# Sums of squares and the spreading of norms placed on column and row tiles of 32

## The chip, the cores and the metric

The kernel runs on one core of one Trainium2 chip, whose engines are TensorE (PE; its weight loads are shown as PEld), VectorE (DVE), ScalarE (ACT), GpSimd (POOL) and SyncE (SP, which issues the large transfers). The metric is device time in microseconds, from the launch to the end of the program. A profiled execution also has a span, from its first to its last instruction.

## The reference, cut to what matters

Three layers follow one another on 256 tokens of width 2048, in fp32. Each is a projection into a wide matrix, a mixer, and a projection back. The first layer's mixer is half sparse attention and half an RWKV recurrence of 16 heads of 64. The second is differential attention with 16 heads, each with two pairs of queries and keys of 64. Three places compute a norm over 64 neighbouring channels, and these are the ones that the change touches:

```python
# layer 1, RWKV: length of the keys, once for each head
kk = (k * k_k.astype(f32)).reshape(B, S, H, N)
kk = kk / jnp.maximum(jnp.sqrt(jnp.sum(kk * kk, axis=-1, keepdims=True)), 1e-12)
...
# layer 1, RWKV: group norm of the output, once for each head
mean = jnp.mean(y, axis=-1, keepdims=True)
var = jnp.mean(jnp.square(y - mean), axis=-1, keepdims=True)
y = ((y - mean) * lax.rsqrt(var + RWKV_GN_EPS)).reshape(B, S, W) * ln_w + ln_b
...
# layer 2: norm of 32 query vectors and 32 key vectors of 64 for each token
q = _rmsnorm(q.reshape(B, S, H, 2, d), qk_g[0]) * (d ** -0.5)
k = _rmsnorm(k.reshape(B, S, H, 2, d), qk_g[1])
```

## The kernel before

Activations lie with channels on partitions and tokens along the free dimension, so a tile is 128 channels by 256 tokens and holds two heads of 64. A norm over 64 channels is therefore a sum over half the partitions, and TensorE makes it. Each of the three norms goes the same way:

1. ACT squares the tiles.
2. **The sums** (`half_sums`, line 98). One matmul for each tile takes a 128-row window of a constant as its stationary operand (all ones in one column for partitions 0 to 63 and in the next column for 64 to 127, zeros elsewhere) and the squares as its moving operand. Shifting the window by two columns puts the sums of tile n in output rows 2n and 2n + 1. The matmuls of one norm accumulate in the same rows of one PSUM bank: 8 rows for the four tiles of RWKV, 32 rows for the 16 tiles of layer 2.
3. DVE and ACT turn these few rows into reciprocal roots: 8 or 32 partitions by 256 elements.
4. **The spread** (lines 970, 1109 and 1670). One matmul for each tile takes a selector (`chosen`, 0 or 1) as its stationary operand, 8 or 32 rows by 128 columns, and the reciprocals as its moving operand. It copies the two rows of that tile to the 128 partitions of its channels.
5. DVE multiplies the tiles by what lies in PSUM (lines 1295, 1395 and 1813).

The selectors are made at run time: POOL copies parts of the identity, each column repeated 64 times, into `chosen` (lines 1460 and 1472 in RWKV, 1917 in layer 2).

Each fp32 matmul appears in the trace as two LDWEIGHTS and two MATMUL instructions, so four such matmuls are a group of x8.

Around this runs the projection (class `Gemm`), which is most of TensorE's work. Weights come by transfers of 512 KB into `w_raw` (issued by SP, line 199, each when DVE has freed a buffer). ACT rounds them to `w_hi` (line 208), DVE makes the rest `w_lo` (line 213), and TensorE multiplies in three steps (lines 241 to 243, or 250 to 252 for the other layout), 256 columns each. TensorE's order is written out by hand: `merged` and `woven` insert the stages of the mixer between slots of the projection, where a slot is three of its matmuls and the lists `stage_slots` and `second_slots` say after which slot a stage comes. ACT and DVE have the same lists. Every engine works through its own order and waits on semaphores.

In RWKV the work comes in two halves (`hh` 0 and 1) of four tiles. `pe_prepare` has the sums of the keys' squares (line 964), the spread (970), the product for the bonus (976) and transposes (987). `pe_finish` has the means (1097), the sums (1102) and the spread (1109). After the second half's last step POOL sets `half_done`, for which SP waits before it loads the weights of the sparse half (line 407).

In layer 2 the function `sums` is called once for each of 16 pairs of tiles, `spread` likewise. Calls 0 to 7 are the queries, 8 to 15 the keys. `roots` on DVE makes the reciprocals of each half. Spreads 8 to 15 follow one another with three slots between them, in `ps` banks 2 and 3 by turns.

Other lines that the text names work on parts of the array already. Lines 1701 and 1702 are the scores of layer 2 with a contraction of 64: the matmuls for one head's t = 0 read partitions 0 to 63 and write bank 0, those for t = 1 read partitions 64 to 127 and write bank 1. Line 2168, in layer 3, has 64 output rows: its blocks b = 0 and 2 (256 and 128 columns) write partitions 0 to 63, b = 1 and 3 (192 and 64 columns) write 64 to 127, with two matmuls for each block. Lines 931 and 932 are two single matmuls, 33 rows by 8 columns into partitions 32 to 39 and 32 rows by 16 columns into partitions 0 to 15.

Of the kernel before, what the change touches and what calls it, by code (L numbers as in the profile page):

```python
# [21 lines left out]
P = 128  # L22
# [34 lines left out]
K_WIN1 = K_WIN2 + 126  # L57
K_END = K_WIN1 + 31

# [7 lines left out]
def constants():  # L67
# [14 lines left out]
    cols.append(np.broadcast_to(np.arange(31) == 15, (P, 31)))  # L82
# [696 lines left out]
def first_layer(k, a, g, xt, following):  # L779
# [14 lines left out]
    small, chosen = ar[0:8, 4096:4352], ar[0:8, 4352:4864]  # L794
    eight = view(con[0:8, K_ID:K_ID + 1], [[1, 8], [0, 64]])
# [13 lines left out]
    def bonus(hh):  # L809
        return k.proj[:, T_ZA:T_ZA + 4, :] if hh == 0 else raw(1, 0)  # L810
# [64 lines left out]
    with ExitStack() as ctx:  # L875
# [13 lines left out]
        f1, f2, th, ug, sg, sc_, md, ce, exd, e1, kr, s2, ss, nr, rn, nb, sl, kn, ka, bo, bp, bn, x1, tq, ev = semaphores(  # L889
            nc, ctx, "rwp", "f1 f2 th ug sg sc md ce ex e1 kr s2 ss nr rn nb sl kn ka bo bp bn x1 tq ev")  # L890
# [16 lines left out]
        def spread(u):  # L907
            return chosen[:, u * P:(u + 1) * P]
# [34 lines left out]
        def pe_prepare(pe, hh):  # L943
# [31 lines left out]
            for q in range(2):  # L975
                mm = pe.matmul(k.ps[:, 2 + q, :], blk, weighted[:, 2 * q:2 * q + 2, :], start=True, stop=True)
# [116 lines left out]
        def pe_finish(pe, hh):  # L1093
# [7 lines left out]
            for u in range(4):  # L1101
                mm = half_sums(k, pe, u, 8, k.ps[0:8, 2, 0:S], ep(hh)[:, u, :], u == 0, u == 3)
            mm.then_inc(vs, 1)
# [3 lines left out]
            pe.wait_ge(sl, 2 * hh + 2)  # L1107
            for u in range(4):
                mm = pe.matmul(k.ps[:, u // 2, (u % 2) * S:(u % 2) * S + S], spread(u), small, start=True, stop=True)
            mm.then_inc(vb2, 1)  # L1110
# [33 lines left out]
        def act_prepare(act, hh):  # L1144
# [32 lines left out]
            nc.scalar.activation(small, k.ps[0:8, 0, 0:S], ACT.Sqrt).then_inc(nr, 1)  # L1177
# [92 lines left out]
        def dve_prepare(dve, hh):  # L1270
# [24 lines left out]
            nc.vector.tensor_tensor(pair(bt(hh)), pair(bt(hh)), k.ps[:, 0:2, :], ALU.mult).then_inc(kn, 1)  # L1295
# [18 lines left out]
            nc.vector.tensor_tensor(pair(bonus(hh)), k.ps[:, 2:4, :], pair(pv), ALU.mult).then_inc(bn, 1)  # L1314
# [65 lines left out]
        def dve_finish(dve, hh):  # L1380
# [8 lines left out]
            nc.vector.tensor_scalar(small, k.ps[0:8, 2, 0:S], 1.0 / 64, 64e-5, ALU.mult, ALU.add).then_inc(ve, 1)  # L1389
# [5 lines left out]
            nc.vector.tensor_tensor(pair(pv), pair(pv), k.ps[:, 0:2, :], ALU.mult).then_inc(yn, 1)  # L1395
# [7 lines left out]
        with nc.Block(no_gpsimd_drain=True) as block:  # L1403
# [23 lines left out]
            def _(pool):  # L1427
# [23 lines left out]
                for hh in range(2):  # L1451
# [8 lines left out]
                    nc.gpsimd.tensor_copy(chosen.rearrange("p (a b) -> p a b", a=8), eight).then_inc(sl, 1)  # L1460
# [10 lines left out]
                    pool.wait_ge(me, hh + 1)  # L1471
                    nc.gpsimd.tensor_copy(chosen.rearrange("p (a b) -> p a b", a=8), eight).then_inc(sl, 1)  # L1472
# [137 lines left out]
def second_layer(k, a, g1, g2, g3, mix, yg, xtok):  # L1610
# [7 lines left out]
    with ExitStack() as ctx:  # L1618
# [18 lines left out]
        rnq = rn[0:32, 0:S]  # L1637
        chosen = [k.proj[0:32, t:t + 4, :].rearrange("p j t -> p (j t)") for t in (T2_V + 4, T2_V + 12)]
# [1012 lines left out]
```

## Time and profile before

| | |
|---|---|
| median of 3 runs | 1797.66 us (1795.15 to 1800.07) |
| profiled execution | span 1793.7 us, its own time not given apart from it; 3.96 us below the median |
| PE busy | 1719.0 us (96%), 13621 matmul instructions |
| PEld busy | 1639.8 us (91%) |
| DVE busy | 1002.4 us (56%) |
| ACT busy | 788.1 us (44%) |
| POOL busy | 97.4 us (5%) |
| mean granted TensorE clock | 0.981 |
| HBM | 140 GB/s over the span |

The busy time of an engine is the union of its instructions. Matmuls overlap one another, so the distance from start to start says what one costs, not its duration. In the timeline "x8" is a group of eight instructions that follow one another, and the figure before the engine is the time from the first one's start to the last one's end. Idle time before a group and its releaser stand in brackets.

### The profile page before, as it was taken

The page shows a single profiled execution, that of the slowest core. Times are in us where ns is not written, and L with a number is a line of the kernel's source. Part 1 is how long each engine was busy: PE and PEld are TensorE (multiplying, and loading weights), DVE is VectorE, ACT ScalarE, POOL GpSimd, SP SyncE. Part 2 cuts the span into 40 slices and gives each one's busy share as a digit, 9 for nine tenths or more (in the row PEclk, how much of TensorE's full clock was granted, in tenths as well). Part 3 has the DMA queues.
Part 4 walks back from the last instruction along what each step waited for, and adds up shares of the span by engine and source line. Part 5 has one row for each costly group of instructions (what it writes and reads, how often), then busy time and mean ns, then how long its engine had stood idle before and what let it go on. Part 6 is the DMA issues. An engine that isn't in the chain of part 4 may idle for free. (4 is left out here: it accounts for less than half of the span.)

```text
span 1793.7 us, 31345 instructions
## 1 busy us (share of the span) xinstructions
PE 1719.0 (96%) x13621; PEld 1639.8 (91%) x13621; DVE 1002.4 (56%) x1273; ACT 788.1 (44%) x1123; POOL 97.4 (5%) x88
## 2 busy tenths in 40 slices
PE   8999999899999898979999999999899999999899
PEld 7989998799998798978999989999898999999899
DVE  5665443664545265466454468887545854455443
ACT  6542223522222355444343348876436434444432
POOL 2210000300000000031000000000011000000000
PEclk9999999899999999989999999999999999999999
DMA  9643232433234915536666534444554655556363
GB/s 283 188 127 94 72 95 60 126 98 92 74 95 120 201 48 172 176 105 174 182 178 168 155 118 139 144 142 153 160 165 135 186 163 146 154 161 181 129 202 104
DMA packets 253584, 254.00 MB, mean 142 GB/s; under 512 B 9153, under 2 KB 249826, under 8 KB 253064
## 3 DMA queue, kind: packets, MB, share of 16 engines
q1 hardware_dynamic: 252792, 251.80, 47.9%
q8 instruction: 107, 1.75, 0.4%
q0 software_dynamic: 656, 0.21, 0.1%
q14 instruction: 29, 0.24, 0.0%
HBM read 249.29 MB, written 2.69 MB: 140 GB/s over the span
## 5 line engine op out<-in xcount | busy, mean ns | idle before, releaser
L213 DVE TENSOR_TENSOR w_lo<-w_raw,w_hi 128x1024 fp32r<-128x1024 f32 (+1 forms) x452 | 550.2, 1220 | 534.1 <-ACT w_hi L208 533.5
L241 PE MATMUL ps<-xt,w_hi 128*128 128x256 f32 x2736 | 805.8, 295 | 24.4 <-DVE w_lo L213 20.5
L242 PE MATMUL ps<-xt,w_hi 128*128 128x256 f32 x2736 | 779.7, 285 | 0.0
L243 PE MATMUL ps<-xt,w_lo 128*128 128x256 f32 x2736 | 779.2, 285 | 0.0
L208 ACT ACTIVATE w_hi<-w_raw 128x1024 fp32r<-128x1024 f32 (+1 forms) x452 | 470.2, 1045 | 667.1 <-PE ps L243 514.9
L241 PEld LDWEIGHTS ps<-xt,w_hi 128*128 128x128 f32 x2736 | 530.0, 194 | 49.5 <-issue 34.8
L242 PEld LDWEIGHTS ps<-xt,w_hi 128*128 128x128 f32 x2736 | 530.6, 194 | 1.2 <-issue 0.7
L243 PEld LDWEIGHTS ps<-xt,w_lo 128*128 128x128 f32 x2736 | 529.9, 194 | 0.0
L250 PE MATMUL ps<-w_hi,xt 128*128 128x256 f32 x832 | 244.0, 293 | 0.0
L251 PE MATMUL ps<-w_lo,xt 128*128 128x256 f32 x832 | 236.8, 285 | 0.0
L252 PE MATMUL ps<-w_hi,xt 128*128 128x256 f32 x832 | 236.6, 284 | 0.0
L250 PEld LDWEIGHTS ps<-w_hi,xt 128*128 128x128 f32 x832 | 161.2, 194 | 8.9 <-issue 7.8
L251 PEld LDWEIGHTS ps<-w_lo,xt 128*128 128x128 f32 x832 | 161.3, 194 | 0.5 <-issue 0.2
L252 PEld LDWEIGHTS ps<-w_hi,xt 128*128 128x128 f32 x832 | 160.9, 193 | 0.0
L319 DVE TENSOR_TENSOR proj<-ps,rs_bc 128x512 f32<-128x512 f32 (+1 forms) x71 | 48.0, 676 | 54.0 <-PE ps L243 53.8
L1052 PE MATMUL ps<-arena 128*128 128x64 f32 (+2 forms) x384 | 46.4, 263 | 0.0
L1052 PEld LDWEIGHTS ps<-arena 128*128 128x128 f32 (+1 forms) x384 | 43.6, 182 | 1.1
L1357 DVE TENSOR_TENSOR arena<-ps,con 128x256 f32<-128x256 f32 (+1 forms) x40 | 21.2, 530 | 38.6 <-PE ps L1042 38.4
L1205 ACT ACTIVATE arena<-ps 128x512 f32<-128x512 f32 x32 | 19.0, 595 | 53.5 <-PE ps L1035 53.3
L1765 ACT ACTIVATE df_sc<-df_sc,df_st 128x128 f32<-128x128 f32 x64 | 28.4, 445 | 7.7 <-DVE df_st L1841 7.6
L1866 DVE RECIPROCAL t_sq<-t_sq 128x256 f32<-128x256 f32 x16 | 27.9, 1746 | 1.0 <-ACT t_sq L1779 1.0
L1472 POOL COPY arena<-con 8x512 f32<-8x512 f32 x2 | 1.3, 667 | 389.7 <-PE ps L1097 389.7
(395 smaller groups left out, 1531.4 us busy)
## 6 DMA issues: line engine op xcount, KB each, us to landing
w_raw<-in_a_w_in SPq DMA_DIRECT2D x128, 512.0 KB, 3.7
w_raw<-in_w_in SPq DMA_DIRECT2D x120, 512.0 KB, 3.6
w_raw<-in_b_w_in SPq DMA_DIRECT2D x96, 512.0 KB, 3.7
w_raw<-in_w_out SPq DMA_DIRECT2D x32, 512.0 KB, 4.2
w_raw<-in_a_w_out SPq DMA_DIRECT2D x32, 512.0 KB, 4.5
w_raw<-in_b_w_out SPq DMA_DIRECT2D x32, 512.0 KB, 3.5
arena<-in_x SPq DMA_DIRECT2D x4, 512.0 KB, 7.1
w_raw<-in_w_in SPq DMA_DIRECT2D x8, 256.0 KB, 3.8
```

What stands on the lines that cost most here:

```text
L208: k.nc.scalar.activation(k.wh[:, p % RING, :, 0:w], k.raw[:, p % RAW, :, 0:w], ACT.Copy).then_inc(k.hi_made, 1)
L213: k.nc.vector.tensor_tensor(k.wl[:, p % RING, :, 0:w], k.raw[:, p % RAW, :, 0:w], k.wh[:, p % RING, :, 0:w].bitcast(F32), ALU.subtract).th ...
L241: pe.matmul(os, h[:, cs], xt[:, kt, 0:S], start=st and ct == 0, stop=False, skip_group_check=True)
L242: pe.matmul(os, h[:, cs], xt[:, kt, S:2 * S], start=False, stop=False, skip_group_check=True)
L243: last = pe.matmul(os, l[:, cs], xt[:, kt, 0:S], start=False, stop=sp, skip_group_check=True)
L250: pe.matmul(os, xh, h[:, 0:w], start=st and tt == 0, stop=False, skip_group_check=True)
L251: pe.matmul(os, xh, l[:, 0:w], start=False, stop=False, skip_group_check=True)
L252: last = pe.matmul(os, xl, h[:, 0:w], start=False, stop=sp, skip_group_check=True)
L319: k.nc.vector.tensor_tensor(spec["dst"], g.bank(c)[:, 0:nt * S].rearrange("p (j t) -> p j t", j=nt), view(k.rsb[:, 0:1], [[0, nt], [1, S]] ...
L1052: m = pe.matmul(share(bank(c, 0), u, lv)[half, :], unit(buf[c][MT], u)[half, half], share(buf[c][QQ], u, lv)[half, :], start=True, stop=True)
L1765: nc.scalar.activation(sc[:, i % 2, t, rows[tt]], sc[:, i % 2, t, rows[tt]], ACT.Exp, bias=st[:, i % 2, 0, t, tt:tt + 1], accum_out=st[:, ...
L1866: nc.vector.reciprocal(rh, rh).then_inc(l4, 1)
```

## The change

The sums of different tiles go to different column tiles of the array. In RWKV tile u takes a stationary operand of 32 columns and writes partitions 32u to 32u + 31 of one bank; of these, rows 32u + 2u and 32u + 2u + 1 hold sums and the rest zeros. The four no longer accumulate. In layer 2 the two tiles of a call write partitions 0 to 31 and 32 to 63, and each of the two accumulates over the eight calls. The steps between run on 128 or 64 partitions instead of 8 or 32, with the same 256 elements on each.

The spreads go to different row tiles: matmul u reads its selector and its reciprocals from partitions 32u to 32u + 31 and writes a bank of its own. In RWKV the selector is a new constant (`K_SEL`, 128 columns, loaded with the others; a constant of 31 columns goes), and POOL's copies fall away. In layer 2 POOL makes the selectors in four copies instead of two, each waiting for the one before. The bonus product moves to banks 4 and 5, and spreads 9, 11, 13 and 15 of layer 2 to banks 0 and 1.

```diff
-K_WIN1 = K_WIN2 + 126
-K_END = K_WIN1 + 31
+K_SEL = K_WIN2 + 126
+K_END = K_SEL + P
...
-    cols.append(np.broadcast_to(np.arange(31) == 15, (P, 31)))
+    cols.append(p % 32 == 2 * (p // 32) + f // 64)
...
-    small, chosen = ar[0:8, 4096:4352], ar[0:8, 4352:4864]
+    small = ar[:, 4096:4352]
...
+        def spread_out(pe, done):
+            for u in range(4):
+                rows = slice(32 * u, 32 * u + 32)
+                mm = pe.matmul(k.ps[:, u, 0:S], con[rows, K_SEL:K_SEL + P], small[rows, :], start=True, stop=True)
+            mm.then_inc(done, 1)
+
+        def row_sums(pe, bank_, squares, done):
+            for u in range(4):
+                mm = half_sums(k, pe, u, 32, k.ps[32 * u:32 * u + 32, bank_, 0:S], squares[:, u, :], True, True)
+            mm.then_inc(done, 1)
...
             pe.wait_ge(s2, hh + 1)
-            for u in range(4):
-                mm = half_sums(k, pe, u, 8, k.ps[0:8, 0, 0:S], bonus(hh)[:, u, :], u == 0, u == 3)
-            mm.then_inc(ss, 1)
+            row_sums(pe, 0, bonus(hh), ss)
             yield
             pe.wait_ge(rn, 2 * hh + 2)
-            pe.wait_ge(sl, 2 * hh + 1)
-            for u in range(4):
-                mm = pe.matmul(k.ps[:, u // 2, (u % 2) * S:(u % 2) * S + S], spread(u), small, start=True, stop=True)
-            mm.then_inc(nb, 1)
+            spread_out(pe, nb)
...
-                mm = pe.matmul(k.ps[:, 2 + q, :], blk, weighted[:, 2 * q:2 * q + 2, :], start=True, stop=True)
+                mm = pe.matmul(k.ps[:, 4 + q, :], blk, weighted[:, 2 * q:2 * q + 2, :], start=True, stop=True)
...
-            nc.scalar.activation(small, k.ps[0:8, 0, 0:S], ACT.Sqrt).then_inc(nr, 1)
+            nc.scalar.activation(small, k.ps[:, 0, 0:S], ACT.Sqrt).then_inc(nr, 1)
...
-            nc.vector.tensor_tensor(pair(bt(hh)), pair(bt(hh)), k.ps[:, 0:2, :], ALU.mult).then_inc(kn, 1)
+            nc.vector.tensor_tensor(bt(hh), bt(hh), k.ps[:, 0:4, 0:S], ALU.mult).then_inc(kn, 1)
...
-                    nc.gpsimd.tensor_copy(chosen.rearrange("p (a b) -> p a b", a=8), eight).then_inc(sl, 1)
...
-                    pool.wait_ge(me, hh + 1)
-                    nc.gpsimd.tensor_copy(chosen.rearrange("p (a b) -> p a b", a=8), eight).then_inc(sl, 1)
...
-        rnq = rn[0:32, 0:S]
-        chosen = [k.proj[0:32, t:t + 4, :].rearrange("p j t -> p (j t)") for t in (T2_V + 4, T2_V + 12)]
+        rnq = rn[0:64, 0:S]
+        chosen = [k.proj[0:64, t:t + 4, :].rearrange("p j t -> p (j t)") for t in (T2_V + 4, T2_V + 12)]
...
-                mm = half_sums(k, pe, m, 32, k.ps[0:32, n // 8, 0:S], dsq[:, u * S:(u + 1) * S], m == 0, m == 15)
+                mm = half_sums(k, pe, m, 32, k.ps[32 * u:32 * u + 32, n // 8, 0:S], dsq[:, u * S:(u + 1) * S],
+                               n % 8 == 0, n % 8 == 7)
             mm.then_inc(ssd2, 1)
+
+        def spread_banks(n):
+            return slice(0, 2) if n > 8 and n % 2 else slice(2, 4)
 
         def spread(pe, n):
             pe.wait_ge(rcd, n // 8 + 1)
-            pe.wait_ge(ch, 2)
-            if n >= 2:
-                pe.wait_ge(xn, n - 1)
+            pe.wait_ge(ch, 4)
+            if n:
+                pe.wait_ge(xn, n if n <= 8 else n - 1)
             for u in range(2):
-                m = 2 * (n % 8) + u
-                mm = pe.matmul(k.ps[:, 2 + n % 2, u * S:(u + 1) * S], chosen[m // 8][:, (m % 8) * P:(m % 8) * P + P],
-                               rnq, start=True, stop=True)
+                m, rows = 2 * (n % 8) + u, slice(32 * u, 32 * u + 32)
+                mm = pe.matmul(k.ps[:, spread_banks(n).start + u, 0:S],
+                               chosen[m // 8][rows, (m % 8) * P:(m % 8) * P + P], rnq[rows, :], start=True, stop=True)
             mm.then_inc(sp2, 1)
...
                 for n in range(2):
-                    nc.gpsimd.tensor_copy(chosen[n].rearrange("p (a b) -> p a b", a=16),
-                                          view(k.con[0:32, K_ID + 16 * n:K_ID + 16 * n + 1], [[1, 16], [0, 64]])).then_inc(ch, 1)
+                    for u in range(2):
+                        rows, at0 = slice(32 * u, 32 * u + 32), K_ID + 32 * u + 16 * n
...
+                        nc.gpsimd.tensor_copy(chosen[n][rows, :].rearrange("p (a b) -> p a b", a=16),
+                                              view(k.con[rows, at0:at0 + 1], [[1, 16], [0, 64]])).then_inc(ch, 1)
```

The group norm's lines (1102, 1109, 1389, 1395) are changed as those of the keys are, and line 1813 reads two half banks instead of one bank.

## Rows read from the trace of the kernel before

**Rows 1.** The page's first line.

```profile
span 1793.7 us, 31345 instructions
```

**Rows 2.** Groups of PE: shapes, count, busy us, mean ns, idle before them and releaser.

```profile
L1670 PE MATMUL ps<-t_sq,proj 32*128 32x256 f32 x64 | 18.0, 400 | 0.0
L98 PE MATMUL ps<-t_sq,con 128*32 128x256 f32 x64 | 16.8, 385 | 0.5 <-ACT t_sq L1741 0.5
...
L98 PE MATMUL ps<-proj,con 128*8 128x256 f32 x32 | 8.6, 418 | 4.3 <-ACT proj L1174 3.3 <-ACT proj L1226 1.0
...
L970 PE MATMUL ps<-arena 8*128 8x256 f32 x16 | 4.0, 387 | 1.1 <-DVE arena L1292 1.1
```

**Rows 3.** Windows of layer 2: length, busy PE, PEld, DVE, ACT, POOL, clock, DMA share, GB/s.

```profile
834.60:1049.00 214.40, 214.40 (x1601) 194.40 (x1601) 100.36 (x96) 75.95 (x82) 1.92 (x4) 1.00 0.60 167
1027.00:1049.80 22.80, 22.80 (x136) 18.11 (x134) 12.62 (x14) 5.26 (x7) 0.00 (x0) 1.00 0.37 116
```

**Rows 4.** Timeline of PE, one call of the sums and one of the spread.

```profile
837.83 1.05 PE L98 MATMUL ps<-t_sq,con 128*32 128x256 f32 x4
838.81 0.39 PE L241 MATMUL ps<-xt,w_hi 128*128 128x256 f32 x1
...
930.63 1.12 PE L1670 MATMUL ps<-t_sq,proj 32*128 32x256 f32 x4
931.68 0.38 PE L241 MATMUL ps<-xt,w_hi 128*128 128x256 f32 x1
```

**Rows 5.** Timeline of PE, the scores of one head in layer 2.

```profile
1061.97 0.50 PE L1701 MATMUL ps<-proj 64*128 64x128 f32 x4
1062.30 0.61 PE L1702 MATMUL ps<-proj 64*128 64x256 f32 x4
1062.84 0.38 PE L250 MATMUL ps<-w_hi,xt 128*128 128x256 f32 x1
```

**Rows 6.** Timeline of PE, one call of line 2168 in layer 3.

```profile
1456.29 1.51 PE L2168 MATMUL ps<-gl_qd,proj 128*64 128x256 f32 x16
1457.73 0.39 PE L241 MATMUL ps<-xt,w_hi 128*128 128x256 f32 x1
```

**Rows 7.** Timeline of PE, lines 931 and 932.

```profile
28.89 0.81 PE L931 MATMUL ps<-arena 33*8 33x384 f32 x2
29.62 0.81 PE L932 MATMUL ps<-arena 32*16 32x384 f32 x2
```

**Rows 8.** Timeline of DVE, then of PE, keys of the first half.

```profile
105.80 2.18 DVE L1290 TENSOR_SCALAR arena<-arena 8x256 f32<-8x256 f32 x1 [0.23 <-ACT arena L1177]
...
109.68 2.28 DVE L213 TENSOR_TENSOR w_lo<-w_raw,w_hi 128x1024 fp32r<-128x1024 f32 x2
...
121.07 1.22 DVE L1314 TENSOR_TENSOR proj<-ps,arena 128x1024 f32<-128x1024 f32 x1
```

```profile
109.81 1.99 PE L970 MATMUL ps<-arena 8*128 8x256 f32 x8 [0.95 <-DVE arena L1292]
...
123.44 0.60 PE L987 MATMUL ps<-con,proj 128*128 128x128 f32 x4
```

**Rows 9.** Timeline of DVE, group norm of the first half.

```profile
312.13 1.23 DVE L213 TENSOR_TENSOR w_lo<-w_raw,w_hi 128x1024 fp32r<-128x1024 f32 x1 [0.46 <-ACT w_hi L208]
314.69 1.22 DVE L1395 TENSOR_TENSOR arena<-arena,ps 128x1024 f32<-128x1024 f32 x1 [1.34 <-PE ps L1109]
```

**Rows 10.** Timeline of DVE, then of POOL, keys of the second half.

```profile
350.54 2.22 DVE L1290 TENSOR_SCALAR arena<-arena 8x256 f32<-8x256 f32 x1 [1.07 <-ACT arena L1177]
```

```profile
350.22 2.39 POOL L1467 TENSOR_TENSOR arena<-arena,proj 128x1024 f32<-128x1024 f32 x1
```

**Rows 11.** Waits of PE, then of SP: us in total, times, longest.

```profile
PE ps L987 <- DVE rw_dec L1310: 0.8, 1, 0.8
```

```profile
SPq L407 <- POOL proj L1474: 21.8, 1, 21.8
```

**Rows 12.** Window in layer 1, columns as in rows 3.

```profile
112.30:115.70 3.40, 3.40 (x18) 3.40 (x17) 3.30 (x4) 0.00 (x0) 0.00 (x0) 0.50 0.86 282
```

More of the change, by code:

```diff
@@ L793, in first_layer @@
     lora = ar[:, 9216:10240]
-    small, chosen = ar[0:8, 4096:4352], ar[0:8, 4352:4864]
-    eight = view(con[0:8, K_ID:K_ID + 1], [[1, 8], [0, 64]])
+    small = ar[:, 4096:4352]
     weighted = ar[:, 5120:6144].rearrange("p (j t) -> p j t", t=S)
@@ L888, in first_layer @@
         n_va, n_vb, n_tab = [0], [0], [0]
[L889 to L890 removed]
+        f1, f2, th, ug, sg, sc_, md, ce, exd, e1, kr, s2, ss, nr, rn, nb, kn, ka, bo, bp, bn, x1, tq, ev = semaphores(
+            nc, ctx, "rwp", "f1 f2 th ug sg sc md ce ex e1 kr s2 ss nr rn nb kn ka bo bp bn x1 tq ev")
         mm_, dv_, ac_ = (semaphores(nc, ctx, "rwc", f"{n}0 {n}1") for n in ("mm", "dv", "ac"))
@@ L905, in post @@
             return (pr, pk, pv)[n]
-        def spread(u):
-            return chosen[:, u * P:(u + 1) * P]
+        def spread_out(pe, done):
[7 more added lines that the diff above has]
+            mm.then_inc(done, 1)
         fills = [(n, tt) for n in range(3) for tt in range(NT)]
@@ L1100, in pe_finish @@
             pe.wait_ge(s3, hh + 1)
-            for u in range(4):
-                mm = half_sums(k, pe, u, 8, k.ps[0:8, 2, 0:S], ep(hh)[:, u, :], u == 0, u == 3)
-            mm.then_inc(vs, 1)
+            row_sums(pe, 2, ep(hh), vs)
             yield
@@ L1106, in pe_finish @@
             pe.wait_ge(yn, 6 * hh + 1)
[L1107 to L1110, printed above, removed]
+            spread_out(pe, vb2)
             yield
@@ L1313, in dve_prepare @@
             dve.wait_ge(bp, hh + 1)
-            nc.vector.tensor_tensor(pair(bonus(hh)), k.ps[:, 2:4, :], pair(pv), ALU.mult).then_inc(bn, 1)
+            nc.vector.tensor_tensor(pair(bonus(hh)), k.ps[:, 4:6, :], pair(pv), ALU.mult).then_inc(bn, 1)
             yield
@@ L1388, in dve_finish @@
             dve.wait_ge(vs, hh + 1)
-            nc.vector.tensor_scalar(small, k.ps[0:8, 2, 0:S], 1.0 / 64, 64e-5, ALU.mult, ALU.add).then_inc(ve, 1)
+            nc.vector.tensor_scalar(small, k.ps[:, 2, 0:S], 1.0 / 64, 64e-5, ALU.mult, ALU.add).then_inc(ve, 1)
             yield
@@ L1394, in dve_finish @@
             dve.wait_ge(vb2, hh + 1)
-            nc.vector.tensor_tensor(pair(pv), pair(pv), k.ps[:, 0:2, :], ALU.mult).then_inc(yn, 1)
+            nc.vector.tensor_tensor(pv, pv, k.ps[:, 0:4, 0:S], ALU.mult).then_inc(yn, 1)
             dve.wait_ge(yn, 6 * hh + 2)
@@ L1806, in roots @@
                     dve.wait_ge(sp2, 8)
-                nc.vector.tensor_scalar(rnq, k.ps[0:32, f, 0:S], 1.0 / 64, EPS, ALU.mult, ALU.add).then_inc(rnd, 1)
+                nc.vector.tensor_scalar(rnq, k.ps[0:64, f, 0:S], 1.0 / 64, EPS, ALU.mult, ALU.add).then_inc(rnd, 1)
                 dve.wait_ge(rsd2, f + 1)
@@ L1812, in scaled @@
                 dve.wait_ge(sp2, n + 1)
-                nc.vector.scalar_tensor_tensor(out=normed(n), in0=normed(n), scalar=gq[:, n // 8:n // 8 + 1],
-                                               in1=k.ps[:, 2 + n % 2, :], op0=ALU.mult, op1=ALU.mult).then_inc(xn, 1)
+                x2 = k.proj[:, 2 * n:2 * n + 2, :]
+                nc.vector.scalar_tensor_tensor(out=x2, in0=x2, scalar=gq[:, n // 8:n // 8 + 1],
+                                               in1=k.ps[:, spread_banks(n), 0:S], op0=ALU.mult,
+                                               op1=ALU.mult).then_inc(xn, 1)
             for _ in range(16):
@@ L1916, in _ @@
                 for n in range(2):
-                    nc.gpsimd.tensor_copy(chosen[n].rearrange("p (a b) -> p a b", a=16),
-                                          view(k.con[0:32, K_ID + 16 * n:K_ID + 16 * n + 1], [[1, 16], [0, 64]])).then_inc(ch, 1)
+                    for u in range(2):
+                        rows, at0 = slice(32 * u, 32 * u + 32), K_ID + 32 * u + 16 * n
+                        if n + u:
+                            pool.wait_ge(ch, 2 * n + u)
+                        else:
+                            pool.wait_ge(a2, 8)
+                        nc.gpsimd.tensor_copy(chosen[n][rows, :].rearrange("p (a b) -> p a b", a=16),
+                                              view(k.con[rows, at0:at0 + 1], [[1, 16], [0, 64]])).then_inc(ch, 1)
                 pool.wait_ge(bi, 2 * SKEW_DONE)
```

## The prediction

> **What bounds the kernel.** I read the page first, then PE's groups, PE's waits, and windows for each stretch. The span is 1793.7 us [rows 1], and PE has work nearly all the time. In layer 2, from 834.6 to 1049.0, it is busy for all 214.40 us, DVE for 100.36 and ACT for 75.95 [rows 3]. Every microsecond taken off PE there comes off the end, if the others keep up. The matmuls that the change touches never waited there except once, for 0.5 us [rows 2]. In layer 1 it is otherwise: the sums waited 4.3 us in all and L970 1.1 us [rows 2], so there chains through ACT, DVE and POOL take over at some places, and each site needs its own account.
>
> **What a group costs now.** Sums of one call in layer 2: four instructions, 0.98 us from their first start to the next projection matmul; a spread 1.05 us [rows 4]. The groups' lengths give the parts. L970's eight take 1.99 us and L1670's four take 1.12 [rows 4, 8]: four more instructions cost 0.87, so 0.216 us each. They run one after the other, at 0.216 us for 256 columns. The rest (0.98 - 4 x 0.216 = 0.12, for a spread 0.19) is the way in and out and stays.
>
> **Does the array run them abreast?** For row tiles the scores say yes. L1701 and L1702 are 4 instructions of 128 columns and 4 of 256: in one stream 4 x 0.108 + 4 x 0.216 + 0.19 = 1.49 us. They took 1062.84 - 1061.97 = 0.87 [rows 5]. Two streams abreast would take half the columns, 0.65 + 0.19 = 0.84. For column tiles L2168 says the same: 16 instructions, 4 x (256 + 192 + 128 + 64) = 2560 columns, in one stream 2.16 + 0.12 = 2.28 us, taken 1.44 [rows 6]; the fuller tile alone, 1536 columns, needs 1.30 + 0.12 = 1.42. So two tiles run abreast at full rate, row tiles in two banks as well as column tiles in one. The excess of 0.02 to 0.03 us I take as the price of the second tile, and for four tiles 0.04. No row shows four abreast, or tiles of 32; I take the same rate, by the nearest rows, and keep "two abreast" and "one after another" as bounds.
>
> Beside this stands the Trainium skill, page "TensorE: Matmul & The Clock Gate", Part 3: it gives four row tiles 3.07 times and three column tiles 2.38 times the speed. By 3.07 an RWKV group would fall from 1.73 to 0.56 us of streaming, 1.17 saved instead of the 1.26 below, as an estimate; eight groups would lose 0.7 us of the sum before cover. No row here has four tiles.
>
> **Layer 2.** 16 sums and 16 spreads each lose two of their four turns: 2 x 0.216 - 0.013 = 0.42 us (0.013 is half of the excess just shown, since a call has one pair and L1701 to L1702 have two). 32 x 0.42 = 13.4 us. Bounds: 0, if they stay in one stream, and 13.8. PE never waits there [rows 3], and the root chain shifts with its input, since the last sum and the spread that needs it move alike. DVE's reads cover the same number of elements. The two extra POOL copies come before the stretch, where POOL has nothing that PE waits for; without that cover they could cost at most two such copies, under 2.5 us (L1917 has two in 2.4 us), and I take nothing.
>
> **Layer 1.** Each of eight groups loses six of eight turns: 6 x 0.216 - 0.04 = 1.26 us, 10.1 in all. What arrives at the end is less:
>
> - *Keys, first half.* The sums end 1.26 earlier, but L1290 ended at 107.98 [rows 8]. Its 2.18 us for 256 elements are a wait behind POOL: in the second half it ends at 352.76, just after POOL's L1467 at 352.61 [rows 10]. So the reciprocals aren't earlier, and PE waits 0.95 + 1.26 us instead of 0.95. The spread's own 1.26 remains for PE. DVE doesn't use it: it has L213 until 111.96, then an unbroken run to the end of L1314 at 122.29 [rows 8]. The third set of transposes, at 123.44, needs that. So at most 123.44 - 122.3 = 1.1 us. I take 1.1 (bounds 0 and 1.3).
> - *Group norm, first half.* Sums 1.26 and spread 1.26 come off PE. L1395 waited 1.34 for the spread after an L213 at 312.13 to 313.36 [rows 9]. That L213 waits for ACT, and ACT for PE, but DVE's reciprocal and the evacuation before it end no earlier than 311.6, so L213 ends at about 312.8 and L1395 moves from 314.69 to there: 1.9 (bounds 1.3 and 2.5). The chain to the next stall of PE hangs on L1395.
> - *Keys, second half.* POOL's copy of 0.60 us is gone, and the root now waits for ACT's table load and no longer for the sums, so L1467 ends 0.6 earlier and L1290 with it. The spread starts 0.6 earlier and takes 1.26 less, 1.9 for PE; L213 on DVE, waiting for its turn, holds L1295 to some 1.6. PE's wait of 0.8 for L1310 [rows 11] shows that DVE's chain counts: 1.6 (bounds 0.6 and 2.5).
> - *Group norm, second half.* The same order on DVE, again 1.7 (bounds 1.3 and 2.5). Behind it SP has waited 21.8 us to issue the sparse weights [rows 11], so all that follows starts earlier by what POOL's L1474 is earlier.
>
> Sum 1.1 + 1.9 + 1.6 + 1.7 = 6.3 us (bounds 3.2 and 8.8). The moved bonus product and the removed copies of `chosen` elsewhere cost and give nothing: it is the same work in free banks. The constants grow by 97 columns, 50 KB in a stretch that moves some 300 GB/s: 0.15 us, within the rounding.
>
> **The sum.** 13.4 + 6.3 = 19.7 us, so a span of 1774.0. The median stands 3.96 us above the profiled span, so 1778.0 us.
>
> **The rivals.**
>
> *Column tiles don't run four or two abreast at a width of 32.* Each streams squares from all 128 partitions; rows show this for two tiles of 64 [rows 6], and nothing for more. Without the sums: 16 x 0.42 = 6.7 goes, and of layer 1 about 2.5. Left 10.5, 1787 us.
>
> *Nothing runs abreast.* The trace would look as before, 1797 us, perhaps 0.6 less for POOL's copy. Rows 5 and 6 speak against it: they would have to hold for 64 and not for 32.
>
> *DVE becomes the bound in the last spreads.* From 1027.0 to 1049.8 DVE has 12.62 us of work in 22.8 [rows 3]. With 8 x 0.42 less the stretch lasts 19.4, still above 12.62, and a spread needs the multiplication two calls back, not the last. If it did bind, those 3.4 us would stay: 1781.4. The Trainium skill, page "TensorEngine Tiling", Performance Considerations, "PSUM Bottleneck", warns of just this: tiling speeds TensorE and not the emptying of PSUM. The numbers just given hold without it.
>
> *Slower: each change of tile empties the array.* From L931 to L932 the tile changes, and 29.62 - 28.89 = 0.73 us passed for two instructions of 384 columns, 0.65 at the rate above [rows 7]; the excess, 0.08 or more, is a drain. If no pair overlapped and each change cost 0.1 to 0.2 us, 32 changes into the second tile in layer 2 and 24 in layer 1 would cost 56 x 0.15 = 8 us: 1806 us. It decides as soon as the overlap fails, for each change above 0.1 us is over 5.4 us in all. Rows 5 and 6 change tiles without such a gap, so I give it little.
>
> *The clock.* After the 8-row spread PE got the 0.50 clock, 1.2 GHz, for 3.4 us [rows 12]; each such stretch costs up to 1.7 us. Fuller use of the array may save one or two, longer waits may add one. This widens the range by 3 us to both sides.
>
> **How the numbers follow.** Forecast (two and four abreast, layer 1 partly covered) 0.76; column tiles fail 0.08; DVE or another chain takes back 3 to 8 us 0.06; nothing abreast 0.05; slower 0.05. A measurement of this kernel tells 0.3%, 5.4 us, from no change. Faster holds the first three cases less a little, 0.89; same 0.06; slower 0.05. Low end: all cover fails, 13.8 + 8.8 + 1.7 for a clock stretch = 24.3, about 1773. High end: the column case at 1787.
>
> **What would show it.** Right: L98 x4 about 0.62 us long, and L1670 x4 about 0.71, instead of 1.05 and 1.12; L98 x8 in RWKV near 0.64, L970 near 0.74, if four run abreast; the wait of PE before L970 in the first half 2.2 us; PE busy throughout layer 2. Wrong: a group of four in RWKV at twice that; a wait of PE in front of L1670 after 1030; sums as long as before while spreads shrink; or stalls in layer 1 that have grown by more than the 3.8 us (10.1 - 6.3) allowed.

## The result, and the profile after

The changed kernel takes 1777.0 us (median of 4, 1775.6 to 1778.0) against 1797.2 before: ratio 0.988, 95% interval 0.987 to 0.990. Forecast were 1778.0 us and a range of 1773 to 1787. The profile page's first line, then two groups of its part 5, in the columns of [rows 2]:

```profile
span 1776.1 us, 31339 instructions
...
L1668 PE MATMUL ps<-t_sq,proj 32*128 32x256 f32 x64 | 11.2, 426 | 0.0
...
L98 PE MATMUL ps<-t_sq,con 128*32 128x256 f32 x64 | 10.0, 391 | 0.5 <-ACT t_sq L1739 0.5
```

L1668 is L1670 of before. As many instructions of the same shape: 18.0 us have become 11.2 and 16.8 have become 10.0, with the mean of one instruction hardly changed. What shrank is therefore not the instruction but the time in which they lie one after the other. The timeline of PE shows single groups: in layer 2 the sums with the projection behind them and the spread, then four tiles in layer 1, first the sums (L98, x8) and then the spread (L909, formerly L970 and L1109):

```profile
832.88 0.62 PE L98 MATMUL ps<-t_sq,con 128*32 128x256 f32 x4
833.44 0.38 PE L241 MATMUL ps<-xt,w_hi 128*128 128x256 f32 x1
...
935.40 0.70 PE L1668 MATMUL ps<-t_sq,proj 32*128 32x256 f32 x4
...
305.25 0.64 PE L98 MATMUL ps<-proj,con 128*32 128x256 f32 x8 [0.33 <-ACT proj L1223]
...
310.32 0.71 PE L909 MATMUL ps<-arena,con 32*128 32x256 f32 x8
310.96 0.39 PE L241 MATMUL ps<-xt,w_hi 128*128 128x256 f32 x1
```

Forecast were 0.62, 0.71, 0.64 and 0.74. Eight instructions in four tiles last hardly longer than four in two. Next, windows from the first sums of layer 2 to its first scores (L1701, now L1699), columns as in [rows 3]; before, then after:

```profile
834.50:1050.76 216.26, 215.42 (x1605) 194.96 (x1605) 101.21 (x97) 76.05 (x82) 1.92 (x4) 1.00 0.60 166
```

```profile
829.98:1032.78 202.80, 201.95 (x1604) 185.85 (x1605) 100.94 (x97) 76.23 (x82) 1.93 (x4) 1.00 0.64 177
1009.50:1031.80 22.30, 22.30 (x161) 17.63 (x160) 13.68 (x16) 6.34 (x8) 0.00 (x0) 1.00 0.42 131
```

Layer 2 is 13.46 us shorter (forecast 13.4), and PE is busy in all but 0.85 us of it, also through the last spreads (second row). So DVE did not become the bound.

In layer 1 the changed kernel was ahead by these amounts (its lead, the difference of the starts of the same instruction in the two traces): 1.1 us at 122 us, 3.1 at 333, 5.8 at 361, 6.6 at 558, where SP is let go. Then the lead shrinks. The chain to L449, the first scores of the sparse attention, gave back 2.0: L449 starts at 617.83 against 622.46, a lead of 4.6. At the end it is 17.6 us. That is 2.6 less than the 20.2 between the medians: the profiled execution of after took 1777.97 us, 1.0 above its median, and that of before was some 1.6 below its own (estimate: its span of 1793.7 and the 1.9 us that lie outside the span in other executions, against 1797.2). The profile's waits name what L449 waits for, here from 575 to 625 us of after; before, the same rows had 8.5 and 5.2:

```profile
DVE cbias L667 <- DMA proj<-bias_rows_dram: 8.9, 1, 8.9
...
PE ps L449 <- DVE arena L623: 5.6, 1, 5.6
```

DVE waits 8.9 us for the last rows of a bias table, has its copies, L319, L213 and L623 still to do, and PE waits 5.6 us for L623. The table's parts are issued by SP in turn with weights. The four issues of the last part, from SP's timeline:

```profile
603.44 1.64 SPq L2545 DMA_DIRECT2D arena<-bias_rows_dram  x1
605.11 0.44 SPq L2546 DMA_DIRECT2D arena<-bias_rows_dram  x1
605.59 0.44 SPq L2545 DMA_DIRECT2D proj<-bias_rows_dram  x1
606.07 0.44 SPq L2546 DMA_DIRECT2D proj<-bias_rows_dram  x1
```

Most issues take 0.43 us; what made the first one 1.64 the trace does not name. The forecast had ended its account of layer 1 at SP's release and did not follow it through this stretch.

### The profile page after: what moved, and what is told of

Same layout as the page of the kernel before. It is cut to its first block and busy times, and to the rows that moved or that the text cites. A ratio compares the mean times of both kernels' runs of the same rounds, so it can differ in the third digit from the quotient of the medians.

```text
span 1776.1 us, 31339 instructions
## 1 busy us (share of the span) xinstructions
PE 1695.2 (95%) x13621; PEld 1623.5 (91%) x13621; DVE 1000.4 (56%) x1273; ACT 790.1 (44%) x1123; POOL 100.6 (6%) x86
## 3 DMA queue, kind: packets, MB, share of 16 engines
q8 instruction: 107, 1.75, 0.4%
## 5 line engine op out<-in xcount | busy, mean ns | idle before, releaser
L213 DVE TENSOR_TENSOR w_lo<-w_raw,w_hi 128x1024 fp32r<-128x1024 f32 (+1 forms) x452 | 550.8, 1221 | 527.3 <-ACT w_hi L208 526.9
L319 DVE TENSOR_TENSOR proj<-ps,rs_bc 128x512 f32<-128x512 f32 (+1 forms) x71 | 48.0, 675 | 53.4 <-PE ps L243 53.3
L1202 ACT ACTIVATE arena<-ps 128x512 f32<-128x512 f32 x32 | 19.0, 595 | 53.5 <-PE ps L1037 53.3
L1468 POOL TENSOR_TENSOR proj<-arena,proj 128x1024 f32<-128x1024 f32 x2 | 5.8, 2908 | 409.1 <-DVE arena L1396 409.1
```

Source lines behind the costliest of these rows:

```text
L213: k.nc.vector.tensor_tensor(k.wl[:, p % RING, :, 0:w], k.raw[:, p % RAW, :, 0:w], k.wh[:, p % RING, :, 0:w].bitcast(F32), ALU.subtract).th ...
L319: k.nc.vector.tensor_tensor(spec["dst"], g.bank(c)[:, 0:nt * S].rearrange("p (j t) -> p j t", j=nt), view(k.rsb[:, 0:1], [[0, nt], [1, S]] ...
```

## The experiments

Each was timed in 4 to 6 runs, beside 9 to 11 runs of the kernel before on the same chip (4 for the changed kernel), whose medians lie from 1795.5 to 1797.9. So kernels of different sets are compared by how far each is below its own before. The last column is the 95% interval of the ratio.

| kernel | median us | below its before | ratio |
|---|---|---|---|
| changed | 1777.0 | 20.2 | 0.987 to 0.990 |
| layer 2 alone changed | 1781.8 | 13.7 | 0.990 to 0.994 |
| layer 1 alone changed | 1789.6 | 5.9 | 0.994 to 0.997 |
| changed, layer 2's sums in turn | 1782.4 | 13.1 | 0.991 to 0.994 |
| changed, layer 2's spreads in turn | 1782.4 | 13.1 | 0.990 to 0.994 |
| changed, layer 1's sums two abreast | 1777.8 | 18.2 | 0.989 to 0.992 |
| changed, layer 1's spreads in turn | 1778.3 | 19.6 | 0.987 to 0.991 |
| changed, bound ahead of the root | 1775.6 | 20.4 | 0.987 to 0.990 |
| changed, one product per norm in layer 2 | 1762.1 | 33.8 | 0.980 to 0.983 |
| changed, table sooner | 1769.7 | 28.2 | 0.981 to 0.986 |
| before, table sooner | 1789.0 | 7.2 | 0.994 to 0.997 |
| one product, bound first | 1761.9 | 36.0 | 0.977 to 0.982 |
| one product, bound first, table sooner | 1752.5 | 45.5 | 0.972 to 0.976 |

### One layer alone

Layer 2 of the changed kernel in the kernel before, and the reverse; no edit inside a layer.

> The kernel before with layer 2's half of the change alone. My theory: the 32 groups of two products each lose one product (0.425 us), 13.4 us in all, between the first sums and the projections that follow, whatever layer 1 does; so about 1783.8 us against 1797.2, and layer 1's product groups as before. Rival: part of the 17.6 us difference between the two profiled executions that belongs to layer 2 comes from stretches at half clock that happen to fall otherwise, and this run gains 16 us or more, or 11 or less.

> The kernel changed, with layer 2's half undone. My theory: layer 1's half is worth about 6.3 us up to the end of its second group norm, in four steps (1.1, 2.0, 2.6 and 0.8 us up to POOL's last addition), and the end is 4.5 to 6.5 us below 1797.2. Rival: of the 6.7 us gained by 582 us only 4.6 remained at 618 us in the changed kernel; if that loss belongs to the change (a stretch at half clock that begins where the second group norm's stall ends sooner), it comes again here and the gain is 4.2 to 4.8 us; if it was chance, the gain is 6.3 us or more.

Measured: 13.7 and 5.9 us, 19.6 together, against 20.2 for both. The window of layer 2, first of the kernel with layer 2 alone changed:

```profile
834.57:1037.37 202.80, 201.95 (x1605) 185.87 (x1605) 100.92 (x97) 75.98 (x82) 1.93 (x4) 1.00 0.65 177
```

then of the one with layer 1 alone:

```profile
832.77:1049.03 216.26, 215.42 (x1605) 194.94 (x1605) 101.24 (x97) 76.28 (x82) 1.92 (x4) 1.00 0.60 166
```

202.80 and 216.26, the lengths of after and before to 0.01 us. Layer 2's share is settled. On layer 1 the median speaks against the rival (4.2 to 4.8), but the interval, 4.7 to 10.1 us, just touches it. In the trace of that run L449 led by 1.9 us, behind a half-clock stretch at 29 us that had cost 4 us, so by 6 without it: of the lead at SP's release, 2.5 and 6.5 without that stretch, 0.6 was lost up to L449, where the changed kernel lost 2.0.

### Layer 2, one half in turn again

```diff
-                mm = half_sums(k, pe, m, 32, k.ps[32 * u:32 * u + 32, n // 8, 0:S], dsq[:, u * S:(u + 1) * S],
-                               n % 8 == 0, n % 8 == 7)
+                mm = half_sums(k, pe, m + 16 * u, 64, k.ps[0:64, n // 8, 0:S], dsq[:, u * S:(u + 1) * S],
+                               m == 0, m == 15)
```

> The kernel changed, but layer 2's sums go into one column tile of 64 that both products of a pair add into, so that they follow each other; row tiles of the spreads stay. My theory: 16 pairs times 0.425 us, 6.8 us more than the changed kernel (about 1783.8 us); each pair takes 1.19 us from the product before to the product behind instead of 0.77. Rival, that the sums were hidden behind ScalarE's squares: under 2 us more. Rival, that a tile switch itself costs something: a column tile of 64 still is a tile, so a price of switching stays in this run and the difference is only the second product.

```diff
-    chosen[m // 8][rows, (m % 8) * P:(m % 8) * P + P], rnq[rows, :], start=True, stop=True)
+    chosen[m // 8][:, (m % 8) * P:(m % 8) * P + P], rnq, start=True, stop=True)
```

> The kernel changed, but layer 2's spreads multiply with a selector of 64 rows that is zero in the other half, so that the two products of a pair follow each other in one row tile of 64; the column tiles of the sums stay. My theory: 16 pairs times 0.425 us, 6.8 us more than the changed kernel (about 1783.8 us); each pair 1.27 us instead of 0.84. Rival, that VectorE's multiplications set the pace of the second half: under 3 us more, with waits of TensorE for VectorE in the changed kernel that shrink here.

Measured: 13.1 us below before instead of 20.2, so 7.1 us lost by each. The windows are sharper. For the sums in turn:

```profile
829.54:1039.51 209.97, 209.12 (x1604) 190.94 (x1604) 101.09 (x97) 76.30 (x82) 1.92 (x4) 1.00 0.63 171
```

for the spreads in turn:

```profile
825.15:1034.77 209.62, 208.78 (x1604) 191.77 (x1604) 101.14 (x97) 76.21 (x82) 1.92 (x4) 1.00 0.62 171
```

Above 202.80 these are 7.17 and 6.82 us, 0.448 and 0.426 for each of 16 pairs (expected 0.425). Both kinds of tile overlap, by equal amounts, and nothing else in layer 2 gained. The two kernels differ by 4 us in where the window starts; that lies ahead of layer 2.

### Layer 1, fewer abreast

```diff
-    mm = half_sums(k, pe, u, 32, k.ps[32 * u:32 * u + 32, bank_, 0:S], squares[:, u, :], True, True)
+    mm = half_sums(k, pe, 17 * u - 32 * c, 64, k.ps[64 * c:64 * c + 64, bank_, 0:S], squares[:, u, :], n < 2, n >= 2)
```

> The kernel changed, but layer 1's four sums of a group lie in two column tiles of 64 with two products each, where the changed kernel has four tiles of 32. My theory, that tiles of one group run abreast and products of one tile in turn: each of the four groups takes 1.06 us instead of 0.63, so 0.43 us each more, 1.7 us in all or a little less where a wait behind absorbs it. Rival: four abreast are not better than two, and nothing changes.

The group took 0.44 us longer, as expected (1.08 against 0.64 above), from PE's timeline of this kernel:

```profile
305.13 1.08 PE L98 MATMUL ps<-proj,con 128*64 128x256 f32 x8 [0.33 <-ACT proj L1225]
```

Of 4 x 0.44 = 1.7 us little arrives in the trace: POOL's last addition starts at 555.84 instead of 555.32, from 0.1 us ahead at the keys. The time, 18.2 us below before instead of 20.2, can't tell 0.6 from 1.7. DVE's timeline shows one place where it goes, for the group norm of the first half, first in the changed kernel:

```profile
310.44 1.21 DVE L213 TENSOR_TENSOR w_lo<-w_raw,w_hi 128x1024 fp32r<-128x1024 f32 x1
311.56 1.21 DVE L1392 TENSOR_TENSOR arena<-arena,ps 128x1024 f32<-128x1024 f32 x1
```

then with the sums two abreast:

```profile
310.31 1.21 DVE L213 TENSOR_TENSOR w_lo<-w_raw,w_hi 128x1024 fp32r<-128x1024 f32 x1
311.44 1.22 DVE L1394 TENSOR_TENSOR arena<-arena,ps 128x1024 f32<-128x1024 f32 x1
```

The multiplication (L1395 of before) starts right behind L213 in both, without the wait of [rows 9]. In the keys' first half PE's wait ahead of L909 shrinks from 2.2 to 1.8 us instead. The keys' second half and the second group norm lose some 0.2 and 0.4. So my expectation priced the group and not what waits for it, and the step from two tiles abreast to four is worth about 0.6 us for all of layer 1's sums.

The spreads in turn, with a selector of 128 rows that is zero outside its 32, which POOL writes four times where `chosen` was written before:

```diff
-    rows = slice(32 * u, 32 * u + 32)
-    mm = pe.matmul(k.ps[:, u, 0:S], con[rows, K_SEL:K_SEL + P], small[rows, :], start=True, stop=True)
+    mm = pe.matmul(k.ps[:, u, 0:S], chosen[:, u * P:(u + 1) * P], small, start=True, stop=True)
```

> The kernel changed, but layer 1's four spreads of a group multiply with selectors of 128 rows that are zero outside their 32, so that they follow each other; POOL writes the selectors again, as before the change (four copies a half, twice). The column tiles of the sums stay. My theory: each of the four groups takes 2.0 us instead of 0.71, 1.28 us more, 5.1 us in all where TensorE's result is waited for at once, less what lies in the waits for VectorE: 3 to 5 us more than the changed kernel. Rival, that the gain of layer 1 came from POOL's copies being gone, not from the row tiles: then the keys' multiplications start later by the copies. Rival, that the spreads' part was hidden: under 1.5 us.

19.6 us below before instead of 20.2, 1778.3 by the median instead of 1777.0: 0.6 or 1.3 us lost where 3 to 5 were expected, and the rival had under 1.5. The group of the first group norm, from PE's timeline, in the kernel before:

```profile
312.46 0.28 PE L243 MATMUL ps<-xt,w_lo 128*128 128x256 f32 x1
312.67 1.99 PE L1109 MATMUL ps<-arena 8*128 8x256 f32 x8
314.59 0.39 PE L241 MATMUL ps<-xt,w_hi 128*128 128x256 f32 x1
```

then with the spreads in turn:

```profile
310.10 0.28 PE L243 MATMUL ps<-xt,w_lo 128*128 128x256 f32 x1
310.22 1.89 PE L910 MATMUL ps<-arena 128*128 128x256 f32 x8
311.76 0.47 PE L241 MATMUL ps<-xt,w_hi 128*128 128x256 f32 x1
312.07 0.28 PE L242 MATMUL ps<-xt,w_hi 128*128 128x256 f32 x1
```

From the start of the projection ahead to that of the one behind it is 1.66 us; in the changed kernel 0.85, before the change 2.13. So the row tiles are worth 1.28 against products in turn in one row tile, as forecast, and only 0.8 to 0.9 against products in turn over the full height. Leaving the full array and coming back costs the rest, 0.47 us up to the first projection behind and 0.39 up to the second, so about 0.4 us a group. I had taken 2.0 us for a group without looking at that. Nor does all of 4 x 0.81 = 3.2 us arrive: nothing is lost in the keys' first half, 0.6 in the first group norm and 0.9 in the keys' second half, so that layer 1's lead at 536 us is 4.3 us instead of 5.8. Another 0.5 is lost up to the start of POOL's last addition, but that takes 2.41 us here and 3.30 in the changed kernel, so at SP's release 1.1 are lost, and 0.6 at the end of the trace. So the rival's number came, in part because the price lay in waits and in part by POOL's shorter addition. POOL's copies are back in this kernel. The keys' multiplications start at 111.84 as in the changed kernel and, in the second half, at 352.15 instead of 350.52, where the sums began 0.6 us later and the group is 0.8 longer: what is lost is the group's, and not the copies'.

### The wait for POOL

```diff
-            act.wait_ge(ss, hh + 1)
-            nc.scalar.activation(small, k.ps[:, 0, 0:S], ACT.Sqrt).then_inc(nr, 1)
+            act.wait_ge(rn, 2 * hh + 1)
+            nc.scalar.activation(small, small, ACT.Sqrt).then_inc(nr, 1)
...
+            dve.wait_ge(ss, hh + 1)
+            nc.vector.tensor_scalar(small, k.ps[:, 0, 0:S], 1e-24, None, ALU.max).then_inc(rn, 1)
             dve.wait_ge(nr, hh + 1)
-            nc.vector.tensor_scalar(small, small, 1e-12, None, ALU.max).then_inc(rn, 1)
-            dve.wait_ge(rn, 2 * hh + 1)
             nc.vector.reciprocal(small, small).then_inc(rn, 1)
```

> The kernel changed, with the lower bound of the key norms applied to the sums (1e-24, by VectorE from PSUM) ahead of ScalarE's root, where the changed kernel applies it to the root (1e-12), behind it. My theory: the bound's 2.18 us in the first half is a wait for the port that VectorE shares with POOL's multiplication, since the same line takes 0.47 us in the second half when it comes ahead of POOL's; from PSUM it takes about 0.4 us, TensorE's wait ahead of the first spreads falls from 2.2 us to about 0.5, and the kernel gains 1 to 2 us. Rival: the reciprocal behind it, which also reads and writes SBUF, inherits the wait, and nothing is gained.

DVE's timeline in the keys' first half, changed kernel:

```profile
105.76 2.18 DVE L1287 TENSOR_SCALAR arena<-arena 128x256 f32<-128x256 f32 x1 [0.23 <-ACT arena L1174]
107.98 1.75 DVE L1289 RECIPROCAL arena<-arena 128x256 f32<-128x256 f32 x1
```

and with the bound first:

```profile
105.02 0.41 DVE L1287 TENSOR_SCALAR arena<-ps 128x256 f32<-128x256 f32 x1
105.92 1.75 DVE L1289 RECIPROCAL arena<-arena 128x256 f32<-128x256 f32 x1 [0.48 <-ACT arena L1174]
```

The same operation takes 0.41 us when it reads PSUM, in the middle of the same POOL instruction, which runs there from 104.10 to 107.37. The reciprocal takes 1.75 us in both, so it doesn't inherit the wait, and the rival is out. PE's wait ahead of L909 falls from 2.2 to 0.6 us, and the trace leads by 3.1 us at 131 us against 1.1. The median is 1.4 us below the changed kernel's and the distance to before 0.2 larger: the time can't tell this gain from none, and only the trace shows it.

### The table's transfers

```diff
     for c in range(P // SKEW):
-        next(parts_a)
-        next(parts_b)
+        for _ in range(2 if c < 4 else 0):
+            next(parts_a)
+            next(parts_b)
         g.load(sp, done + 7 + c)
```

> The kernel changed, with another order of SyncE's transfers after the second group norm: two parts of the bias table ahead of each of four weight pieces, and then four weight pieces, in place of one part ahead of each of eight. In the changed kernel the last part is issued at 606.1 us and VectorE waits for the table until 614.6 us, TensorE 5.6 us behind it (until 617.8). My theory: layer 1's gain is partly spent here, since the time from the second half's end to the table is set by the transfers; four weight pieces of 0.5 MB less ahead of the table bring it 5 us or more sooner, TensorE's wait falls to 1 us or less, and the kernel gains 3 to 5 us. Rival, that the transfers behind are late in their turn: TensorE waits for the weights that were moved back, and nothing is gained. Rival, that the table was never what TensorE waited for: L449 starts at 617 us again.

> The kernel before the change, with the parts of the bias table sooner, as in the kernel changed with that order. If the wait for the table is a property of both kernels (TensorE waited 5.2 us for it before the change, 5.6 after), the gain is much the same here as there, 5 to 7 us, 1789 to 1792 us. Rival: the wait is something that the change brought about, and the kernel before gains 2 us or less.

Measured 1769.7, 28.2 us below before instead of 20.2, so 8 us gained where 3 to 5 were expected, and 1789.0, 7.2 us below the kernel before (expected 5 to 7). The spans shrank by 6.7 and 6.6. Waits from 575 to 625 us of the changed kernel with the new order:

```profile
DVE cbias L668 <- DMA proj<-bias_rows_dram: 1.5, 1, 1.5
```

and PE's timeline there, where L450 is L449 of the others:

```profile
611.67 0.28 PE L243 MATMUL ps<-xt,w_lo 128*128 128x256 f32 x1
611.79 0.38 PE L450 MATMUL ps<-proj 128*128 128x128 f32 x2
```

No wait of PE is left ahead of the scores, which start 6.0 us sooner. So the table's wait is real, it is in both kernels, and the weights moved back did not come too late: up to 830 us PE waits for `w_lo` for 4.5 us in either order, and its other waits add up to 0.7 us more. Whether the 2.0 us that the changed kernel lost there belong to the change is not shown. The lead at L449 over the kernel before was 4.6 us in the changed kernel, 4.5 with layer 2's sums in turn, and 7.6 with layer 2's spreads in turn, kernels whose layer 1 is the same. From SP's release to DVE's first copy of the table it took 53.9 us before and 54.5 in the kernel with layer 2 alone changed; with the changed layer 1 it took 55.9, 55.7 and 53.3 in the three just named and 54.5 in the kernel with layer 1 alone changed. So kernels with one and the same layer 1 lie 2.6 us apart there, more than the loss.

### One product for a norm

Layer 2 leaves sum and spread and multiplies each pair's squares with the ones of a block of 64, 512 columns in one product; root and reciprocal are then of 128x512, 16 times.

```diff
-                mm = half_sums(k, pe, m, 32, k.ps[32 * u:32 * u + 32, n // 8, 0:S], dsq[:, u * S:(u + 1) * S],
-                               n % 8 == 0, n % 8 == 7)
...
-                mm = pe.matmul(k.ps[:, spread_banks(n).start + u, 0:S],
-                               chosen[m // 8][rows, (m % 8) * P:(m % 8) * P + P], rnq[rows, :], start=True, stop=True)
...
+            pe.matmul(k.ps[:, n % 2, :], k.con[:, K_BLK:K_BLK + P], dsq, start=True, stop=True).then_inc(ssd2, 1)
```

> The kernel changed, but layer 2 takes sum and spread in one product of 512 columns per pair with the constant of ones in each block of 64, and root and reciprocal are taken of all 128 rows. TensorE needs 16 times about 0.86 us instead of 16 times 0.77 + 0.84, 12 us less; ScalarE gets 16 roots of 128x512 and VectorE 16 reciprocals of 128x512. My theory: VectorE's reciprocals at some 3.4 us each (estimate, from the 1.7 us of a 128x256 one) are more than a pair's share of the projections' time allows in the second half, so the gain is between 0 and 11 us. Rival: the elementwise work becomes the bound and the kernel is slower than the changed one by 5 us or more.

1762.1, 33.8 us below before, 13.6 more than the changed kernel, where 0 to 11 were expected. The window of layer 2 and DVE's and PE's groups:

```profile
828.16:1019.47 191.31, 191.11 (x1508) 183.09 (x1508) 148.54 (x109) 84.76 (x96) 1.92 (x4) 1.00 0.65 183
```

```profile
L1654 PE MATMUL ps<-t_sq,con 128*128 128x512 f32 x32 | 16.5, 597 | 0.7 <-ACT t_sq L1731 0.7
...
L1794 DVE RECIPROCAL t_sq<-t_sq 128x512 f32<-128x512 f32 x16 | 53.5, 3347 | 0.0
```

Layer 2 is shorter by 11.5 us than in the changed kernel (12 expected), all that PE saves. The 53.5 us of reciprocals, which I had feared as the bound, fit: DVE is busy for 148.5 of 191.3. PE streams two instructions of 512 columns for a pair. The tiled way takes as long for its columns, 512 for the sums and 512 for the spread once two are abreast, but it leaves the full array and comes back twice. The 11.5 us are 0.72 for each pair, about twice the 0.4 of a row group above, so this way in and out would explain them; for column tiles alone no run measures it. The other 2 us of the 13.6 lie outside this window and can't be put down to the edit: in the trace the window already starts 1.8 us sooner than the changed kernel's (828.16 against 829.98), behind a stretch in which the two kernels differ only by POOL's copies of `chosen`.

### Together

> Both edits in one kernel: the norms of layer 2 by one product with the ones of a block, and the key norms' bound ahead of the root. They lie 700 us apart and share nothing, so the gains should add: 1762.1 less about 2 us, 1760 us. Rival: the second one's gain is lost in the transfers between the layers, and the time stays at 1762.

> The same with the bias table's parts sooner, as well. By my theory of the table 3 to 5 us below the kernel without it, about 1756 us; by the rival no less than that one.

1761.9 and 1752.5 us, 36.0 and 45.5 below before. The bound ahead of the root adds 2.2 us to the 33.8, but by the median itself only 0.2 (1762.1 and 1761.9), which is what the rival had, and the intervals of the two overlap: not decided by the times. In the traces it adds 2.0 us of lead behind the keys' first half, of which 1.0 is left at 536 us. The table's order adds 9.5, more than the 3 to 5 I had given it. The last kernel is 2.6% faster than the one before, and 25 us ahead of the changed one.

## Why the prediction was right

- *Abreast at width 32, two and four.* Right to 0.03 us a group. A spread of four tiles fell by 1.28 us from projection to projection (2.13 to 0.85), so by the 1.26 of the sum and not by the 1.17 of the estimate beside it. The tiles of a group start 6 to 8 ns apart, less than the 13 taken. The page "TensorE: Matmul & The Clock Gate" of the Trainium skill, Part 3, gives "4ns" for this; the trace measures 6 to 8, nearly always 6 or 7.
- *Layer 2, 13.4 us.* Measured 13.46 in the window, and again with layer 2 alone; undone by halves, its two edits cost 7.2 and 6.8.
- *Layer 1, 6.3 us up to SP's release.* Measured 6.6. Its terms: keys first half 1.1 (forecast 1.1), group norm 2.0 (1.9), keys second half 2.6 (1.6), group norm 0.8 (1.7). The third was too small: I had DVE's bound wait for POOL again, 0.6 us earlier. It came 0.29 us ahead of POOL's multiplication instead and took 0.47 us. The fourth was right for the start of POOL's last addition, 1.7 us, but that took 3.30 us in place of 2.42. In the changed kernel it started 0.16 us behind an L213 of DVE (555.16 to 556.37); before, 0.41 us ahead of one. That it waited for DVE is my reading of these starts; no run tests it. So the third term was 1.0 too small and the fourth 0.9 too large, and that their sum came out to 0.3 us is luck. The two rows on the third, of DVE and of POOL in the changed kernel:

```profile
346.62 0.47 DVE L1287 TENSOR_SCALAR arena<-arena 128x256 f32<-128x256 f32 x1 [0.47 <-ACT arena L1174]
```

```profile
346.91 2.43 POOL L1463 TENSOR_TENSOR arena<-arena,proj 128x1024 f32<-128x1024 f32 x1
```

The rows on the fourth, POOL's last addition before and after:

```profile
562.81 2.42 POOL L1474 TENSOR_TENSOR proj<-arena,proj 128x1024 f32<-128x1024 f32 x1 [13.45 <-DVE arena L1399]
```

```profile
555.32 3.30 POOL L1468 TENSOR_TENSOR proj<-arena,proj 128x1024 f32<-128x1024 f32 x1 [202.63 <-DVE arena L1396]
```

- *From there to the end* the forecast had nothing but a wider range. 2.0 us were lost at the table, and the clock moved the lead by 1.5 us up and 1.8 down: before had 0.50 from 1051.0 to 1054.4 where after had 1.00; after had 10.2 us of it from 1241.5 where before had 6.8 from 1262.6 (0.7 us lost), and 6.8 from 1354.1 where before had 3.4 from 1375.2 (1.1 lost). In all the half clock (1.2 GHz) held for 68 us before and 65 after. The 3 us for the clock that the prediction adds to both sides are not in its bounds: the low end has 1.7 of them, the high end none. Windows of before, then of after, columns as in [rows 3]:

```profile
1051.00:1054.40 3.40, 3.40 (x18) 2.75 (x17) 1.97 (x3) 1.07 (x2) 0.00 (x0) 0.50 0.00 0
1262.60:1269.40 6.80, 4.46 (x21) 4.49 (x22) 6.80 (x7) 6.32 (x7) 0.00 (x0) 0.50 0.46 143
1375.20:1378.60 3.40, 3.40 (x10) 2.66 (x9) 2.54 (x8) 1.06 (x1) 0.00 (x0) 0.50 0.52 159
```

```profile
1033.10:1036.50 3.40, 3.40 (x32) 3.07 (x29) 2.69 (x4) 2.12 (x2) 0.00 (x0) 1.00 0.00 0
1241.50:1251.70 10.20, 6.14 (x29) 6.17 (x30) 8.75 (x8) 8.28 (x9) 0.96 (x1) 0.50 0.41 130
1354.10:1360.90 6.80, 5.61 (x13) 4.54 (x14) 4.64 (x12) 0.92 (x1) 0.00 (x0) 0.50 0.28 84
```

In the first row of each, the same place of the work, PE ran 18 instructions at 0.50 and 32 at 1.00.
- *The 3.96 us between span and median.* This step was wrong by 2 us. It took the distance of one execution's span from the median of others for what lies outside a span; where time and span of one execution are both known, that is 1.8 to 1.9 us in every one. The profiled execution of before was a fast one. The span of after came out 2.1 us above the forecast 1774.0, and the two errors cancel: that the median was met to 1.0 us is in part luck. Between the medians 20.2 us were gained for the 19.7 of the sum, between the two traces 17.6.
- *The rivals.* Column tiles in turn, nothing abreast and a cost for each change of tile are refuted by the groups above. DVE as the bound is refuted by the window to 1031.8. What there is of a tile change, 0.4 us into and out of a tile mode, was in before as well and cancelled.

## What to carry over

Products that use 32 or 64 rows or columns of the array ran abreast here when they lay side by side, two as well as four, and where TensorE never waits the saving could be added up from a few rows (13.4 us forecast, 13.46 measured); where it does, price what waits for the group, not the group. Compare tiles with the full array too: one full-height product in place of two tiled groups was worth more here. Follow a gain through the next transfer on which an engine waits in order, for a table queued between weights can cost more than the arithmetic.

## What the runs showed that I had not expected

- A group in row tiles pays about 0.4 us for leaving the full array and coming back: 2.13 us before the change against 1.66 for the same eight instructions over the full height, so 0.47, and 0.39 up to the second projection instruction behind. The Trainium skill, page "TensorEngine Tiling (Array Packing)", Key Properties, says that a change of mode drains the array; 0.4 us is a size for it here, for products of 256 columns, as far as these rows tell.
- DVE's lower bound from SBUF to SBUF took 2.18 us in the changed kernel and ended at 107.94, with POOL's TENSOR_TENSOR (first row below), and 0.41 when it read PSUM. With layer 1's spreads in turn it took 0.47 us in the middle of POOL's TENSOR_SCALAR (POOL's row, then DVE's). DVE's L213, which reads two operands from SBUF, took 1.23 us beside the TENSOR_SCALAR (from 344.92, changed kernel) and 2.52 beside a TENSOR_TENSOR (from 349.40, layer 1's spreads in turn). So of POOL's instructions only one kind was seen to hold DVE up. The page "Advanced Engine Details and Errata" of the Trainium skill, VectorE Performance Modes, says that GPSIMD instructions and DVE's two-port ones block each other, without a difference between kinds.

```profile
104.53 3.27 POOL L1466 TENSOR_TENSOR arena<-arena 128x1024 f32<-128x1024 f32 x1
```

```profile
344.00 4.48 POOL L1463 TENSOR_SCALAR arena<-arena,va 128x256 f32<-128x256 f32 x4
```

```profile
347.23 0.47 DVE L1288 TENSOR_SCALAR arena<-arena 128x256 f32<-128x256 f32 x1 [0.47 <-ACT arena L1175]
```

- Moving four weight pieces of 0.5 MB behind a table was worth 7 to 8 us by the medians in both kernels, 6.6 to 6.7 by the spans, as much as all of layer 1's tiles or more.
